# Differential attention of a two-block transformer: three pairs of score banks, and maps combined before they are normalized

## The reference, cut to what matters

```
s = einsum('bqhcd,bkhcd->bhcqk', q_blk, k[:, :n_k]) * scale
s = where(kpos <= qpos, s, -inf)
p = softmax(s, axis=-1)
a = p[:, :, 0] - lam * p[:, :, 1]
o = einsum('bhqk,bkhe->bqhe', a, v[:, :n_k])
o = rms_norm(o, sub_gain) * (1 - lam_init)      # over the 128 columns of a head, eps 1e-6
```

## Time and profile before

| what | us |
|---|---|
| median of three runs | 3144.57 |
| profiled execution, whole | 3139.92 |
| its span | 3138.0 |
| TensorE busy | 2925.7 (93%) |
| VectorE busy | 1729.9 (55%) |
| ScalarE busy | 1222.5 (39%) |
| GpSimd busy | 1105.0 (35%) |
| stage `diff`, last exit of the panels (1489.67) to first matmul of the projection (1620.24) | 130.57 |
| in that stage: TensorE busy | 86.58 |
| VectorE busy | 89.80 |
| ScalarE busy | 66.42 |
| mean granted TensorE clock, whole span and stage | 0.97 and 0.89 of full |

### The profile page before, as it was taken

The page is one execution under the profiler, slowest core; times in us unless marked ns, Lnnn a source line. Parts: engine busy times, 40 slices in busy tenths (PEclk is TensorE's granted clock), DMA queues, the critical chain, the costliest instruction groups (busy, mean ns, idle before and its releaser), DMA issues.

```text
span 3138.0 us, 39991 instructions
## 1 busy us (share of the span) xinstructions
PE 2925.7 (93%) x13704; PEld 2385.4 (76%) x13704; DVE 1729.9 (55%) x2176; ACT 1222.5 (39%) x2056; POOL 1105.0 (35%) x484
## 2 busy tenths in 40 slices
PE   5989999999879999999679999999899998999999
PEld 4767778877657888888458888888777897788887
DVE  7575757474546553764755333576275726563333
ACT  2564432233544322344443222466445654332221
POOL 3311444443214444443224444444202431044443
PEclk9998999998989999999889999999899999999999
DMA  5243445451002333332013333232102220033332
GB/s 195 83 150 124 154 128 194 141 160 63 28 21 81 94 100 94 89 94 88 1 34 94 95 98 96 88 95 89 48 1 62 88 88 8 15 100 94 94 94 94
DMA packets 364859, 278.85 MB, mean 89 GB/s; under 512 B 13363, under 2 KB 320948, under 8 KB 363700
## 3 DMA queue, kind: packets, MB, share of 16 engines
q1 hardware_dynamic: 363472, 276.76, 28.8%
q10 hardware_dynamic: 1251, 0.33, 0.0%
HBM read 274.96 MB, written 2.10 MB: 88 GB/s over the span
## 4 chain that ended last, share of the span: by engine, by line
PE 62%; issue 6%; DVE 3%; ACT 2%; POOL 1%; DVEq 0%; ACTq 0%; POOLq 0%
PE banks L993 12%; PE banks L988 12%; PE banks L997 12%; PE banks L945 6%; PE banks L951 6%; PE banks L948 6%; PE banks L1173 1%; PE banks L920 1%; PE banks L1355 1%; PE banks L1287 1%; PE banks L990 1%; ACT tmp L1777 0%; PE banks L1162 0%; PE banks L1335 0%; ACT tmp L1906 0%
## 5 line engine op out<-in xcount | busy, mean ns | idle before, releaser
L815 POOL TENSOR_TENSOR w_lo<-w_raw,w_hi 128x1024 fp32r<-128x1024 f32 (+1 forms) x424 | 1046.2, 2468 | 1831.2 <-ACT w_hi L1484 1830.2
L1484 ACT ACTIVATE w_hi<-w_raw 128x1024 fp32r<-128x1024 f32 (+1 forms) x424 | 445.6, 1051 | 1126.9 <-PE banks L997 824.0
L945 PE MATMUL banks<-w_hi,h_hi 128*128 128x512 f32 x960 | 387.5, 404 | 10.5 <-ACT h_hi L1661 7.2
L948 PE MATMUL banks<-w_hi,h_lo 128*128 128x512 f32 x960 | 378.7, 394 | 3.7 <-DVE h_lo L511 3.7
L951 PE MATMUL banks<-w_lo,h_hi 128*128 128x512 f32 x960 | 379.1, 395 | 0.8 <-POOL w_lo L815 0.7
L988 PE MATMUL banks<-h_hi,w_hi 128*128 128x512 f32 x1280 | 340.2, 394 | 10.0 <-ACT h_hi L1668 9.8
L993 PE MATMUL banks<-h_lo,w_hi 128*128 128x512 f32 x1280 | 319.3, 390 | 1.6 <-DVE h_lo L511 1.6
L988 PEld LDWEIGHTS banks<-h_hi,w_hi 128*128 128x128 f32 x1280 | 242.6, 190 | 65.6 <-issue 13.9
L997 PE MATMUL banks<-h_hi,w_lo 128*128 128x512 f32 x1152 | 284.5, 389 | 0.0
L993 PEld LDWEIGHTS banks<-h_lo,w_hi 128*128 128x128 f32 x1280 | 240.2, 188 | 55.2 <-DVE h_lo L511 5.7
L997 PEld LDWEIGHTS banks<-h_hi,w_lo 128*128 128x128 f32 x1152 | 216.2, 188 | 44.9
(11 more groups left out here) (311 smaller groups left out, 4505.4 us busy)
## 6 DMA issues: line engine op xcount, KB each, us to landing
w_raw<-in_m_w_up SPq DMA_DIRECT2D x64, 512.0 KB, 3.9
w_raw<-in_m_w_down SPq DMA_DIRECT2D x64, 512.0 KB, 3.4
Z<-in_ada_w SPq DMA_DIRECT2D x48, 512.0 KB, 4.7
w_raw<-in_kv_w SPq DMA_DIRECT2D x48, 512.0 KB, 3.7
w_raw<-in_ffn_w_gate SPq DMA_DIRECT2D x44, 512.0 KB, 3.8
w_raw<-in_ffn_w_up SPq DMA_DIRECT2D x44, 512.0 KB, 3.8
tmp<-in_ada_w SPq DMA_DIRECT2D x32, 512.0 KB, 4.8
w_raw<-in_ffn_w_down SPq DMA_DIRECT2D x32, 512.0 KB, 3.4
```

Source lines behind the costliest of these rows:

```text
L815: pool.tensor_tensor(wlo[j][:, 0:n], raw[j][:, 0:n], whi[j][:, 0:n], ALU.subtract).then_inc(s_wlo, 1)
L945: pe.matmul(t, hh, wh, start=k == 0, stop=False)
L948: pe.matmul(t, hl, wh, start=False, stop=False)
L1484: act.activation(whi[par][:, 0:kc * P], raw[par][:, 0:kc * P], ACT.Copy).then_inc(s_whi, 1)
```

## The change

The diff, cut to its core:

```diff
         def diff_scores(s, c):
-            return bank[2 * (s % 2) + c]
+            return bank[2 * (s % 3) + c]
...
@@ GpSimd: high parts of head 0 are left to ScalarE; fewer rows are zeroed
-                for h in range(8):
+                for h in range(1, 8):
+                    pool.wait_ge(e["high_parts"], past(3 * h))
...
+                elif kind == "diff":
+                    todo = [qk[64:128, 5 * S:6 * S], qk[64:128, 7 * S:8 * S], qk[0:64, 9 * S:10 * S], qk[0:64, 11 * S:12 * S]]
...
@@ TensorE
-                zero_rows_in(2)
                 def scores(s):
                     pe.wait_ge(e["low_parts"], past(3 * h + 3))
-                    pe.wait_ge(e["probs"], past(2 * s - 2))
+                    if s == NB:
+                        zero_rows_in(4)
+                    pe.wait_ge(e["probs"], past(2 * s - 4))
...
                 def turn_map(s):
-                    pe.wait_ge(e["taken"], past(s - 1))
+                    pe.wait_ge(e["taken"], past(s))
+                    pe.wait_ge(e["log_mean"], past((s + BEHIND - NB) // NB))
                     for kb in range(b + 1):
-                        mm = pe.transpose(bank[4 + s % 2][...], diff_probs(s, 0)[...], ident)
+                        mm = pe.transpose(bank[6][...], diff_probs(s, 0)[...], ident)
...
                 def mean_square(h):
                     pe.wait_ge(e["squares"], past(h + 1))
-                    pe.wait_ge(e["log_mean"], past(h))
-                    pe.matmul(bank[7], ones, zt(28), start=True, stop=True).then_inc(e["mean_square"], 1)
+                    pe.wait_ge(e["taken"], past(min(NB * h + 2 * NB - BEHIND, DIFF_SLOTS)))
+                    pe.wait_ge(e["eps_scaled"], past(h + 1))
+                    pe.matmul(bank[6], ones, zt(28), start=True, stop=False, skip_group_check=True)
+                    for s in range(NB * h, NB * h + NB):
+                        _, b = diff_slot(s)
+                        mm = pe.matmul(bank[6][:, b * P:(b + 1) * P], diff_eps(s).to_broadcast([P, P]), ident, start=False, stop=s == NB * h + NB - 1, skip_group_check=True)
+                    mm.then_inc(e["mean_square"], 1)
 
+                scores(0)
+                scores(1)
                 for s in range(DIFF_SLOTS + BEHIND):
-                    if s < DIFF_SLOTS:
-                        scores(s)
                     h, i = divmod(s, NB)
+                    if s >= BEHIND:
+                        turn_map(s - BEHIND)
                     if i == NB - 1 and h:
                         mean_square(h - 1)
-                    if s >= BEHIND:
-                        turn_map(s - BEHIND)
-                        if i == (BEHIND - 1) % NB and h:
-                            values(h - 1)
+                    if s + 2 < DIFF_SLOTS:
+                        scores(s + 2)
+                    if i == (BEHIND - 1) % NB and h and s >= BEHIND:
+                        values(h - 1)
...
@@ ScalarE
+                act.activation(q_hi[0], zt(0), ACT.Copy).then_inc(e["high_parts"], 1)
+                for r, t in zip(HALF, k_hi):
+                    act.activation(t[0][r, :], zrows(r, 8), ACT.Copy).then_inc(e["high_parts"], 1)
                 for s in range(DIFF_SLOTS + BEHIND):
                     h, i = divmod(s, NB)
                     if i == NB - 1 and h:
                         square(h - 1)
+                    if i == 0 and h >= 2:
+                        scale(h - 2)
                     if s >= BEHIND:
                         take_map(s - BEHIND)
                     if s < DIFF_SLOTS:
                         probs(s)
-                    if i == NB - 1 and h:
-                        scale(h - 1)
-                    if i == 1 and h >= 2:
+                    if i == 2 and h >= 2:
                         y_high(h - 2)
...
@@ VectorE
                 def combine(s):
-                    dve.reciprocal(inv, diff_small(s, 1)).then_inc(e["inverted"], 1)
-                    dve.tensor_scalar(second, second, inv[:, 1:2], lamv, ALU.mult, ALU.mult).then_inc(e["second_scaled"], 1)
-                    dve.scalar_tensor_tensor(first, first, inv[:, 0:1], second, ALU.mult, ALU.subtract).then_inc(e["combined"], 1)
+                    dve.reciprocal(inv, l2).then_inc(e["inverted"], 1)
+                    dve.scalar_tensor_tensor(ratio, inv, minus_lam, l1, ALU.mult, ALU.mult).then_inc(e["ratio"], 1)
+                    dve.scalar_tensor_tensor(first, second, ratio, first, ALU.mult, ALU.add).then_inc(e["combined"], 1)
...
+                def scale_eps(h):
+                    dve.scalar_tensor_tensor(diff_eps(NB * h, NB), l1, P * EPS, l1, ALU.mult, ALU.mult).then_inc(e["eps_scaled"], 1)
...
-                low_q(0)
-                low_k(0, 0)
-                low_k(0, 1)
+                first_parts()            # two memsets of 64 x 1024, then low_q(0), low_k(0, 0), low_k(0, 1)
+                neg_max(0)
                 for s in range(DIFF_SLOTS + 1):
                     h, i = divmod(s, NB)
-                    if s < DIFF_SLOTS:
-                        neg_max(s)
+                    if s + 1 < DIFF_SLOTS:
+                        neg_max(s + 1)
                     if s:
                         combine(s - 1)
-                    if i == 0 and h >= 2:
+                    if i == 0 and h:
+                        scale_eps(h - 1)
+                    if s == 0:
+                        low_q(1)
+                        low_k(1, 0)
+                    if i == 0 and h < 7:
+                        low_k(h + 1, 1)
+                    if i == 1 and h >= 2:
                         sub_norm(h - 2)
-                    if i == 1 and h < 7:
-                        low_q(h + 1)
-                    if i >= 2 and h < 7:
-                        low_k(h + 1, i - 2)
-                    if i == 2 and h >= 2:
+                    if i == 2 and h < 6:
+                        low_q(h + 2)
+                    if i == 3 and h < 6:
+                        low_k(h + 2, 0)
+                    if i == 3 and h >= 2:
                         sub_low(h - 2)
+                sub_norm(6)
                 sub_low(6)
```

More of the change, by code:

```diff
@@ L136, in program @@
         small = sb("small", [P, 64])
-        lamv = small[:, 0:1]
+        minus_lam = small[:, 0:1]
         m2 = small[:, 48:48 + 4 * GROUPS]
@@ L694, in diff_scores, with diff_neg_max, diff_sums, diff_ratio @@
         def diff_scores(s, c):
-            return bank[2 * (s % 2) + c]
+            return bank[2 * (s % 3) + c]
         def diff_probs(s, c):
             return tmp[2 * (s % 4) + c]
-        def diff_small(s, what):
-            return sums8[:, 8 * what + 2 * (s % 4):8 * what + 2 * (s % 4) + 2]
+        def diff_neg_max(s):
+            return sums8[:, 2 * (s % 4):2 * (s % 4) + 2]
+        def diff_sums(s, n=1):
+            return sums8[:, 8 + 2 * (s % 8):8 + 2 * (s % 8) + 2 * n]
+        def diff_ratio(s):
+            return sums8[:, 24 + 2 * (s % 2):25 + 2 * (s % 2)], sums8[:, 25 + 2 * (s % 2):26 + 2 * (s % 2)]
+        def diff_eps(s, n=1):
+            return sums8[:, 28 + s % 8:28 + s % 8 + n]
         block = ctx.enter_context(nc.Block())
@@ L1344, in turn_map @@
                     pe.wait_ge(e["combined"], past(s + 1))
-                    pe.wait_ge(e["taken"], past(s - 1))
+                    pe.wait_ge(e["taken"], past(s))
+                    pe.wait_ge(e["log_mean"], past((s + BEHIND - NB) // NB))
                     for kb in range(b + 1):
-                        mm = pe.transpose(bank[4 + s % 2][:, kb * P:(kb + 1) * P], diff_probs(s, 0)[:, kb * P:(kb + 1) * P], ident)
+                        mm = pe.transpose(bank[6][:, kb * P:(kb + 1) * P], diff_probs(s, 0)[:, kb * P:(kb + 1) * P], ident)
                     mm.then_inc(e["turned"], 1)
@@ L1354, in values @@
                     for kb in range(NB):
-                        mm = pe.matmul(bank[6][:, kb * P:S], zt(16 + h)[:, kb * P:(kb + 1) * P], zt(24 + kb)[:, kb * P:S],
+                        mm = pe.matmul(bank[7][:, kb * P:S], zt(16 + h)[:, kb * P:(kb + 1) * P], zt(24 + kb)[:, kb * P:S],
                                        start=kb == 0, stop=kb == NB - 1, skip_group_check=True)
@@ L1920, in square @@
                     act.wait_ge(e["mean_square"], past(h))
-                    act.activation(zt(28), bank[6], ACT.Square).then_inc(e["squares"], 1)
+                    act.activation(zt(28), bank[7], ACT.Square).then_inc(e["squares"], 1)
                 def scale(h):
@@ L1926, in scale @@
                     act.wait_ge(e["rms_scale"], past(h))
-                    act.activation(zt(29), bank[7], ACT.Ln, bias=eps, scale=1.0 / P).then_inc(e["log_mean"], 1)
+                    act.activation(zt(29), bank[6], ACT.Ln, scale=1.0 / P).then_inc(e["log_mean"], 1)
                     act.wait_ge(e["log_mean"], past(h + 1))
@@ L2057, in _ @@
             dve.wait_ge(av, 4)
-            link(dve.scalar_tensor_tensor(lamv, small[:, 42:43], LAM_INIT, small[:, 43:44], ALU.add, ALU.subtract))
```

(10 more changed lines are left out.)

30 lines of the change are left out of this document (18 added, 12 removed).

## The result

After the change the median of 5 runs is 3126.41 us (3124.96 to 3127.89), before it 3144.57 (3141.83 to 3146.23, 5 runs): ratio 0.9943, interval 0.9929 to 0.9958, so 18 us faster. The forecast was 3133.5 in a range of 3124 to 3142: right in sign and range, 7 us too high.

What follows compares the result with a forecast made beforehand. No engine is full; a chain of waits through late `low_k` and the head's border bounds a head. Gains 5.4 + 5.65 + 2.1 - 0.1 - 2.0 = 11 us, taken from the median, give 3133.5, range 3124 to 3142.

Steps and rivals of the forecast that it cites:

- first scores: Start of the stage: VectorE zeroes itself, ScalarE copies beside it, so the first scores start at 1495.0, 2.6 us earlier.
- values 5 to values 6: Near the stage's end: values of head 6 need no scores before them, 11.0 us after head 5's, before 13.1; gain 2.1.
- values 6 to values 7: Near the stage's end: three maps turned and copied in turn through one bank, 9.05 us, before 8.92; loss 0.1.
- A head in the middle: Chain from mean square to mean square: 12.55 us against 13.68, 1.13 less for each of five heads, 5.65 in all.
- Epsilon matmuls: TensorE at the head's border: 4 x 128 columns, the same as the mean square, add 0.96 us a head.
- The rival of a slow broadcast load: Rival 3: the broadcast stationary operand loads slowly, eight records at 0.5 us, 13 us slower, 3157.5; chance 0.07.
- The third pair: Score banks in a middle head: TensorE's wait, 1.05 us, for an exponent to free one of two bank pairs goes.
- The first head: VectorE is the bound there; values of head 0 at 1513.3 us, before 1518.69: gain 5.4, weakest term, 3 to 8.
- The end: Values of head 7 to the stage's end: TensorE at its lower level again, epsilon matmuls add nearly 2.09 us; loss 2.0.
- `sub_norm` is waited for by `y_high` alone: In a middle head, the norm comes a slot later and only `y_high`, last in its slot, waits for it.
- The distance to the median: Median of shown runs is 4.65 us above the profiled execution (3139.92); the same 11 off it gives 3133.5.
- Rival 1: VectorE is what counts, the border's chain is looser: a head of 10.7 us, 20 gained in all, 3124.5; chance 0.1.

## Why the prediction was right

| step | forecast | measured |
|---|---|---|
| first scores | 2.6 | 2.7 |
| values of head 0, in all | 5.4 | 2.9 |
| five heads | 5.65 | 6.45 |
| values 5 to values 6 | 2.1 | 2.0 |
| values 6 to values 7 | -0.1 | -0.2 |
| values 7 to the end | -2.0 | +0.8 |
| stage | 11 | 12.0 |

- **A head in the middle** was read from the right chain, and each of its steps came within 0.2. The moved `low_k` removes TensorE's wait of 1.32, shown from both sides: `low_k` late costs the whole gain and more in the stage, `low_k` early alone takes before's first two heads to 11.95.
- **Epsilon matmuls:** 0.96 forecast, 0.90 measured, and on the path. The rival of a slow broadcast load is out.
- **The third pair:** the forecast had it remove the wait on one of two pairs. A wait of 0.83 for exponents is still there, and two pairs gave shorter heads at full clock. What the third pair and the new order bought together is heads at full clock, which the forecast did not price: with both, the unnormalized maps and their 0.98 a head included, the stage is 2.65 shorter than with `low_k` and the start alone. Whether the order would do it with two pairs is not shown.
- **The first head was the weak term,** 2.5 too high. About 1.0 of it is VectorE meeting GpSimd, which was not counted: 512 columns were combined in 1.15, where before's took 0.75 in the mean, the epsilon product took 0.56 and not 0.15, and 256 columns 0.78 and not 0.48. About 1.45 is the last scores ahead of the values, 3.2 from 1514.37 to 1517.57: I took 1.75 for them, a row at full clock, and the granted clock of that stretch is 0.50.
- **The end was wrong in sign.** The values took 4.00, slow as forecast, but the clock was back at 2.4 GHz for the mean square and the epsilon matmuls: 1.12 and 1.05, not twice 2.09. "I expect the lower level again" held for one of the three steps. The miss here and the one in the first head cancel, which is luck.
- **"`sub_norm` is waited for by `y_high` alone" was false.** The values wait for it too. In after it ends 0.15 ahead of them and costs nothing, but with two other orders it costs 0.5 and 0.6 a head. The margin was luck.
- **The distance to the median:** I took the same 11 from the median as from the profiled execution. The medians moved by 18.2: 1.0 of the 7 that the forecast is off is the stage, the other 6 lie in what surrounds it and in the choice of the execution. With the stage's 12.0 alone the time would have been 3132.6.
- **Rival 1 named a time, 3124.5,** that is nearer than mine, by another mechanism: a head of 10.7, and it is 12.40. Taking VectorE's work as the bound would have kept the unnormalized maps, which cost 0.98 a head.

## What to carry to other kernels

Where no engine is full, read the ring of waits from one turn to the next and price every instruction on it: 1.0 us off the busiest engine was worth nothing, 0.9 us onto the ring cost 0.9 in every turn. A bank or tile that is written again has all its readers as waiters, so list the margin of each, not of the one that was last. Read the granted clock of every turn before two orders are compared: a shorter chain, 11.95 at full clock, took 13.65 in most of its turns. The longest idle time of TensorE did not tell which order would keep its clock, for 1.57 kept it in the kernel before and 1.44 lost it here. And compare stages, not whole times, where the rest of a program moves by more than the gain.

## What the runs showed of the hardware

- A float32 matmul of 128 columns with one column broadcast as its stationary operand is two records, 0.112 apart, with weight loads of 0.190, as those of full tiles (0.192 for line 1335).
- A VectorE instruction with two inputs in SBUF can be slowed when GpSimd casts beside it: 512 columns combined take 0.75 alone and 0.99 to 1.17 beside casts, and even one element a partition 0.65 in place of 0.22, until the cast ends. It can also be the casts that are drawn out: two took 2.16 from 1512.63 and 1.28 from 1505.86 in the kernel after, while `low_k` beside the slow ones took its usual 0.69. The norm, with one of its inputs in PSUM, took 0.74 beside casts and 0.75 alone. By the Trainium skill, "SBUF — State Buffer", section "Who interferes with whom", VectorE's second port pair is shared with GpSimd and only that pair makes them contend. The trace agrees: VectorE's memsets, which read nothing, took 0.91 each beside GpSimd's own, no more than the 0.97 worked out from one that stood alone.
- The granted clock can settle into a fall in every turn of a loop of 13.6 us with no idle time above 1.5 (the kernel before with the early `low_k`, five turns in a row), and a loop with an idle time of 1.57 in each turn can keep full clock (the kernel before). One execution of a kernel can have a fall in a turn where two others have none (4.11 in place of 2.42 for the values of head 1).
